# Branch C's output gate of tokens 256-511 computed feature by feature inside the lookup loop, and seven of sixteen lookups weighed by DVE in the first units

## The chip, the cores and the metric

One core of one Trainium2 chip. The metric is the device time of one execution in microseconds; the kernel before was run three times. All arithmetic is in float32: a matrix product of two operands of this type shows in the trace as two MATMUL records (passes).

## What is computed

One layer of a transformer-like trunk on 512 tokens of width 1024:

```
n = adaLN(RMSNorm(x), c)
ya, yb, yc = sparse attention(n), stick-breaking attention(n), gated linear attention(n)
   yc = rms_norm(o) * gain * silu(r),    r = n @ w_cr        (512 columns: the output gate of branch C)
merged = sum_b sigmoid(n @ G_b + bias_b) * (y_b @ w_o_b)
h = x + gate1 * (merged @ w_out)
n2 = adaLN(RMSNorm(h), c)
out = h + gate2 * sum over 8 heads, 16 experts: softmax * gelu(n2 . u[expert]) * v[expert]
```

The last line is the lookup part. Each of the 4 tiles of 128 tokens has 8 heads, and each head picks 16 experts per token out of 16384. A lookup (number n, 0 to 511) gathers one expert for each token of a tile: 128 rows of 8 KB, u and v side by side, 1 MB. 16 lookups of one head and tile are a unit (0 to 31); 4 lookups are a slot (0 to 127) of the order in which all other work is strewn into the loop.

## The kernel before, in words

Everything is written out by hand: each engine runs one long program, and semaphores order them. Stages:

1. Modulation, norm, transposition (to some 95 us), then the projections. `jobs_of_projection` lists the jobs: "d" gives features on partitions, "t" tokens on partitions. Jobs of kind "rc" (slot 7 of the weights, w_proj 7, 2 MB) compute r, one for each tile of 128 tokens, 8 products of 128x128 by 512 columns (L665). Before the change there are four.
2. Branch A for tokens 0-255 (`for it in range(NA + 5)`, 21 turns). `job_after(it)` puts one of the projection jobs after every odd turn, until all but the last four (`LATE = 4`) are done: turns 17 and 19 hold the jobs rc 0 and rc 1. The weights stream through three slots in a fixed order; w_proj 7 takes the slot of w_proj 6 and can be issued by SP only when PE has used that. After turn 17's job come the column sums (L599), 64 narrow products that finish the modulation; in turn 19 branch A's output is turned (L749).
3. Branch B (`for it in range(HB + 2)`) starts with the product of L806. Behind it stand three of the last four jobs (cu 0 and cu 1, the decay projection, L676, and rc 2), and in turn 2 the last (rc 3). Gate and output products of the merge (`gate_product`, L770, and `out_product`, L784), for tokens 0-255, are put between.
4. Branch C for all tokens. Silu of r on ACT (L1393), times the gain on POOL (L2211), times the normed output on DVE (L1878), then PE turns it (L926).
5. The rest of the merge and W_out for tokens 0-255, norm, the first queries.
6. The lookup loop. For each lookup: POOL issues the gather (L2238) into a slot of a ring (8 slots until lookup 120, then 10, up to 15), DVE forms the dot product (L2071), ACT the gelu (L1504), DVE the weight (L2080). Then either PE weighs the row (`weigh`: ACT writes a diagonal matrix, L1515, PE two products of 512 columns, L1121) or DVE does (L2095, two halves of 512). `on_dve(n)` says which: lookups 6, 9, 12, 15 of a unit, and also 1 and 3 in the units 1 to 7 and 9 to 15. The slot of the ring is free when the row is weighed.

Into the loop are strewn, by slot: branch A for tokens 256-511, the queries and scores of further heads (`QUERY_SLOT`: the product in that slot and the next, the score in the second after it; ACT copies it, DVE picks the 16 experts of unit u + 2 in unit u), and the merge for tokens 256-511 (`MERGE_SLOT`, 24 items: branch and 128 features each). A merge item is `merge_products` on PE (8 gate products L1023 into bank 6, 4 output products L1028 into bank 7, 256 columns each), `half_gate` on ACT (Tanh, L1458) and, one slot later, `half_merge` on DVE (L1914 to L1918). SP loads its weights, 768 KB, three items ahead (L538), and the weights of a query, 1152 KB, two slots ahead of it (L532). Pieces of W_out follow in slots 39 to 42.

At the end the last weights and the last weighing are followed by `finish`: bank + DVE's sum (L2110), times gate2 (L2112), plus h (L2115), and a store of 512 KB.

```
def job_after(it):
    return J_A + it // 2 if it % 2 == 1 and J_A + it // 2 < NJ - LATE else None

def half_unit(n):
    return (n // KT + 1) % 3, n % KT
```

Of the kernel before, what the change touches and what calls it, by code (L numbers as in the profile page):

```python
# [7 lines left out]
ALU = mybir.AluOpType  # L8
# [5 lines left out]
P = 128  # L14
# [28 lines left out]
V_C, V_BMOD, V_G1, V_G2, V_BG, V_BA, V_GAIN, V_ONG = 0, 8, 56, 64, 72, 96, 98, 102  # L43
# [59 lines left out]
def jobs_of_projection():  # L103
# [16 lines left out]
def encoder_layer(nc, cst, vec, x, x_turned, w_mod, w_proj, w_small, w_alpha, w_merge, w_out, w_pq,  # L120
                  uv_table, out):
    with ExitStack() as ctx:
# [159 lines left out]
        ON_DVE, ALSO_DVE = (6, 9, 12, 15), (1, 3)  # L282
# [173 lines left out]
        QUERY_SLOT = {(44 if q == 10 else 4 * (q - 3) + 1): q for q in range(3, 11)}  # L456
# [3 lines left out]
        def half_unit(n):  # L460
            return (n // KT + 1) % 3, n % KT
# [15 lines left out]
        def unit_of(t, h):  # L477
# [4 lines left out]
            [4, 7, 8, 11, 12, 15, 16, 19, 20, 22, 23, 24, 26, 27, 28, 29, 30, 31, 32, 33, 34, 35, 36, 37])}  # L482
# [3 lines left out]
        LATE_QUERY_AT = {2: 2, 4: 3}  # L486
# [9 lines left out]
        def _(sp):  # L496
# [37 lines left out]
            def merge_weights(n):  # L534
                br, c = half_unit(n)
                if n >= 3:
                    sp.wait_ge(s["mh_used"], n - 2)
                sp.dma_start(mh_slot[n % 3], w_merge[3 * br + c // 3][:, UNIT_W * (c % 3):UNIT_W * (c % 3 + 1)])\  # L538
                  .then_inc(mh_in[n % 3], 16)
# [22 lines left out]
            for slot in range(NL // GROUP):  # L562
                if slot in MERGE_SLOT and MERGE_SLOT[slot] + 3 < NG:
                    merge_weights(MERGE_SLOT[slot] + 3)
# [5 lines left out]
                if slot == 38:  # L570
                    sp.wait_ge(s["mh_used"], NG)
# [6 lines left out]
            for t in range(TT):  # L578
                sp.wait_ge(s["added"], t + 1)
                sp.dma_start(out[P * t:P * (t + 1), :], h_tm(t)).then_inc(s["stored"], 16)  # L580
            sp.wait_ge(s["stored"], 16 * TT)
# [13 lines left out]
        def _(pe):  # L595
# [375 lines left out]
            def query(q, c):  # L971

                h, lo, n = QUERIES[q]
                if c == 0:
# [5 lines left out]
                    if q == 10:  # L980
                        pe.wait_ge(s["yg_ready"], 8)
# [31 lines left out]
            def merge_products(n):  # L1013

                br, c = half_unit(n)
# [5 lines left out]
                pe.wait_ge(s["gate_ready"], NG + n)  # L1021
                for k in range(KT):
                    mm = pe.matmul(bank(6, H), w[:, P * k:P * (k + 1)], n_t[:, k, H:T],  # L1023
                                   start=(k == 0), stop=(k == KT - 1))
                mm.then_inc(s["gl_done"], 1)
                pe.wait_ge(s["gate_used"], NG + n)
# [7 lines left out]
            def output_piece(p):  # L1034

                pe.wait_ge(wo_in[p % 2], 16 * (p // 2 + 1))
                if p == 0:
                    pe.wait_ge(s["gate_used"], 2 * NG)
                    pe.wait_ge(s["ot_out"], TT)
                    pe.wait_ge(s["q_out"], 10)  # L1040
# [1254 lines left out]
```

## Time and profile before

| | |
|---|---|
| three runs, median (lowest, highest) | 2041.88 us (2039.61, 2043.86) |
| the profiled execution, its time | 2041.46 us |
| its span, first to last instruction | 2039.7 us |
| mean granted TensorE clock | 0.910 of full speed |
| busy: PE, DVE, ACT, POOL | 1670.9, 1443.5, 579.5, 632.1 us |
| moved by DMA | 659.79 MB, of which 536.90 MB by the gathers |

How to read it: the times come from unprofiled and profiled executions; the rows come from one profiled execution, so a sum of rows is set against 2041.46, and what lies outside the span is 1.8 us. Busy shares are means over stages that have different limits.

### The profile page before, as it was taken

How to read it: one execution, taken by the hardware profiler on the slowest of the kernel's cores; microseconds unless marked ns; L12 is line 12 of the kernel's file. 1: busy time of each engine (PE TensorE's matmuls, PEld its weight loads, DVE VectorE, ACT ScalarE, POOL GpSimd, SP SyncE). 2: the span in 40 equal slices, each digit the busy share in tenths (PEclk: the TensorE clock that was granted, in tenths of full speed). 3: DMA queues.
4: the chain of work that ended last, by engine and by line, in shares of the span. 5: the costliest groups of instructions: out<-in, count | busy, mean ns of one | idle time of the engine just before them, and what ended most of it. 6: DMA issues, size and time to landing. Idle time of an engine off the chain costs nothing.

```text
span 2039.7 us, 17878 instructions
## 1 busy us (share of the span) xinstructions
PE 1670.9 (82%) x5626; PEld 946.5 (46%) x5626; DVE 1443.5 (71%) x3353; ACT 579.5 (28%) x1272; POOL 632.1 (31%) x542
## 2 busy tenths in 40 slices
PE   4999989999998898999888867777877676667676
PEld 3533446667786565556555523334433222222222
DVE  5353642668328788887778899878777878887876
ACT  2111114664224253442211223222222222222221
POOL 0000001110003433334333545444444544445441
PEclk8999998999999999999899978878898988888888
DMA  9633020221449999999999999999999999999995
GB/s 375 250 131 118 7 88 10 77 93 57 163 177 372 385 419 419 401 398 406 406 420 420 419 417 405 421 419 419 420 420 421 420 419 420 420 419 419 420 419 228
DMA packets 89183, 659.79 MB, mean 323 GB/s; under 512 B 9968, under 2 KB 10240, under 8 KB 15488
## 3 DMA queue, kind: packets, MB, share of 16 engines
q0 software_dynamic: 73728, 536.90, 63.9%
q1 hardware_dynamic: 14768, 120.75, 15.0%
q8 instruction: 45, 0.74, 0.1%
q10 hardware_dynamic: 592, 0.98, 0.1%
q14 instruction: 50, 0.41, 0.1%
HBM read 655.52 MB, written 2.82 MB: 323 GB/s over the span
## 4 chain that ended last, share of the span: by engine, by line
PE 41%; DMA 34%; DVE 12%; issue 7%; ACT 4%; POOL 2%; SPq 0%; DVEq 0%; POOLq 0%; PEldq 0%; ACTq 0%
DMA sb<-uv_table,sb 33%; PE ps L1121 11%; PE ps L663 6%; PE ps L665 4%; PE ps L770 3%; PE ps L984 3%; DVE sb L2071 2%; DVE sb L2095 2%; POOL sb L2238 2%; PE ps L1023 2%; PE ps L1028 2%; PE ps L784 1%; PE ps L949 1%; DMA sb<-w_mod 1%; PE ps L1047 1%
## 5 line engine op out<-in xcount | busy, mean ns | idle before, releaser
L1121 PE MATMUL ps<-sb 128*128 128x512 f32 x1424 | 774.1, 689 | 273.0 <-ACT sb L1515 269.3
L2238 POOL DMA_INDIRECT sb<-uv_table,sb x512 | 605.1, 1182 | 870.9 <-PE ps L1121 657.4
L2071 DVE CUSTOM_DVE_ANT_0 sb<-sb 128x1024 f32<-128x1024 f32 x512 | 625.2, 1221 | 248.1 <-DMA sb<-uv_table,sb 240.1
L1121 PEld LDWEIGHTS ps<-sb 128*128 128x128 f32 x1424 | 292.3, 217 | 695.2 <-ACT sb L1515 392.0
L1515 ACT ACTIVATE sb<-sb 128x128 f32<-128x128 f32 x356 | 132.0, 397 | 607.1 <-DVE sb L2080 602.1
L2095 DVE SCALAR_TENSOR_TENSOR sb<-sb 128x512 f32<-128x512 f32 x304 | 214.7, 748 | 2.2
L1504 ACT ACTIVATE sb<-sb 128x2 f32<-128x2 f32 x256 | 51.7, 202 | 396.3 <-DVE sb L2071 396.2
L2200 POOL TENSOR_TENSOR sb<-sb 128x128 f32<-128x128 f32 x8 | 13.1, 1636 | 422.8 <-DVE sb L1776 422.8
L663 PE MATMUL ps<-sb 128*128 128x512 f32 (+1 forms) x304 | 125.2, 563 | 0.1
L984 PE MATMUL ps<-sb 128*128 128x256 f32 (+1 forms) x576 | 117.8, 359 | 0.3 <-issue 0.3
L984 PEld LDWEIGHTS ps<-sb 128*128 128x128 f32 x576 | 100.5, 197 | 30.8 <-issue 20.4
L665 PE MATMUL ps<-sb 128*128 128x512 f32 x192 | 93.1, 641 | 6.7 <-DMA sb<-w_proj 6.7
L770 PE MATMUL ps<-sb 128*128 128x256 f32 x384 | 91.5, 392 | 7.0 <-ACT sb L1326 3.0
L1023 PE MATMUL ps<-sb 128*128 128x256 f32 x384 | 87.2, 379 | 2.5 <-ACT sb L1458 2.5
L663 PEld LDWEIGHTS ps<-sb 128*128 128x128 f32 x304 | 57.1, 194 | 62.1 <-issue 55.4
L770 PEld LDWEIGHTS ps<-sb 128*128 128x128 f32 x384 | 73.3, 195 | 20.5 <-ACT sb L1326 3.4
L1023 PEld LDWEIGHTS ps<-sb 128*128 128x128 f32 x384 | 71.5, 189 | 19.9 <-issue 10.7
L665 PEld LDWEIGHTS ps<-sb 128*128 128x128 f32 x192 | 38.7, 206 | 56.2 <-issue 48.4
L1028 PE MATMUL ps<-sb 128*128 128x256 f32 x192 | 51.3, 414 | 14.1 <-DVE sb L1918 13.7
L1566 ACT ACT_TABLE_LOAD x43 | 55.2, 1283 | 0.7
L1028 PEld LDWEIGHTS ps<-sb 128*128 128x128 f32 x192 | 38.8, 207 | 23.5 <-DVE sb L1918 16.8
L1647 DVE SCALAR_TENSOR_TENSOR sb<-sb 128x4096 f32<-128x4096 f32 x7 | 31.4, 4483 | 22.4 <-DMA sb<-w_mod 22.0
(281 smaller groups left out, 1776.7 us busy)
## 6 DMA issues: line engine op xcount, KB each, us to landing
sb<-w_mod SPq DMA_DIRECT2D x11, 2048.0 KB, 9.6
sb<-w_pq SPq DMA_DIRECT2D x18, 1152.0 KB
sb<-w_merge SPq DMA_DIRECT2D x24, 768.0 KB
sb<-w_proj SPq DMA_DIRECT2D x8, 2048.0 KB, 8.9
sb<-w_merge SPq DMA_DIRECT2D x6, 2304.0 KB, 9.0
sb<-w_out SPq DMA_DIRECT2D x8, 1024.0 KB, 10.5
sb<-uv_table,sb POOLq DMA_INDIRECT x512, 27.7
sb<-w_merge SPq DMA_DIRECT2D x3, 1536.0 KB, 6.5
```

The source lines that it names most:

```text
L663: mm = pe.matmul(bank(b, n), w[:, i, k, :], n_t[:, k, 0:n], start=(k == 0), stop=(k == KT - 1))
L665: mm = pe.matmul(bank(b), n_t[:, k, P * i:P * (i + 1)], tiles(views[slot], KT)[:, k, :], start=(k == 0), stop=(k == KT - 1))
L770: mm = pe.matmul(gate_at(n), w[:, P * k:P * (k + 1)], n_t[:, k, 0:H], start=(k == 0), stop=(k == KT - 1))
L984: mm = pe.matmul(bank(6 if q < EARLY_Q else 4, n, H * c), w[:, c, k, :], n_t[:, k, lo:lo + n], start=(k == 0), stop=(k == KT - 1))
L1023: mm = pe.matmul(bank(6, H), w[:, P * k:P * (k + 1)], n_t[:, k, H:T], start=(k == 0), stop=(k == KT - 1))
L1028: mm = pe.matmul(bank(7, H), w[:, P * (KT + k):P * (KT + k + 1)], y_of(br, 1)[:, k, :], start=(k == 0), stop=(k == 3))
L1121: mm = pe.matmul(bank(2 * (t % 2) + f), dgw[m % NDG], row_v(n)[:, T * f:T * (f + 1)], start=(i == 0), stop=(i == PH * PK - 2))
L1515: act.activation(dgw[m % NDG], ident, ACT.Copy, scale=wgt[n // PK % 2][:, n % PK:n % PK + 1])\
L1566: act.activation(warm, cact[:, 0:1], ACT.Gelu)
L2071: dve.tensor_tensor_reduce(out=row_u(n), in0=row_u(n), in1=n2_tm(u // PH), scale=1.0, scalar=0.0, op0=ALU.mult, op1=ALU.add, accum_out=dot ...
L2095: ins = dve.scalar_tensor_tensor(acc_v[f], v, wgt[u % 2][:, i:i + 1], acc_v[f], ALU.mult, ALU.add)
L2238: pool.indirect_dma_start(out=ring[PLACE[n]], out_offset=None, in_=uv_table, in_offset=bass.IndirectOffsetOnAxis(ap=experts[u % 4][:, i:i ...
```

## The change

Five edits, in one version.

- r is projected for tokens 0-255 alone: two of the four "rc" jobs go, and the last four jobs are now rc 0, cu 0, cu 1, rc 1. Silu, gain and product of branch C's end take the first 256 tokens alone. yc of tokens 256-511 is turned without its gate.
- Its gate comes as four new items of the merge list (`ITEMS`, now 28). A gate item loads 512 KB from a new input w_rc, makes 8 products as a merge item does (no output products), Tanh without bias, and two operations on DVE: (tanh + 1) * r from bank 6, then yc = yc * (0.5 * gain) * that. `MERGE_SLOT` is new: gate items in slots 8, 12, 16, 20, each two slots ahead of the next merge item, 28 slots from 6 to 37. Before, it held 24 slots from 4 to 37. Branch 2 (yc) comes after the gates.
- Queries 8, 9, 10 (tokens 128-255 of heads 0 to 2) move from slots 21, 25, 44 to 42, 46, 50. Late query 2 moves from slot 2 to 3.
- In units 1 to 7 DVE weighs lookups 1, 3, 6, 9, 11, 13, 15 (7 of 16), in the last unit 2, 5, 8, 10.
- The end: gelu, weight and diagonal of the last two lookups are made singly. DVE multiplies its own sum by gate2 and adds h while the last rows come (`own_part`, `own_rest`), and `finish_last` works and stores in two halves of 512 columns.

```diff
-    jobs += [("t", 7, t, "rc", None) for t in range(TT - 2)]
+    jobs += [("t", 7, 0, "rc", None)]
     jobs += [("u", None, i, "cu", None) for i in range(2)]
-    jobs += [("t", 7, t, "rc", None) for t in range(TT - 2, TT)]
+    jobs += [("t", 7, 1, "rc", None)]
...
+        ON_DVE, ALSO_DVE, LAST_DVE, FIRST_DVE = (6, 9, 12, 15), (1, 3), (2, 5, 8, 10), (1, 3, 6, 9, 11, 13, 15)
...
+            if u == NU - 1:
+                return i in LAST_DVE
+            if 0 < u < PH:
+                return i in FIRST_DVE
             return i in ON_DVE or (i in ALSO_DVE and u % PH > 0 and n < 2 * PH * PK)
...
-        QUERY_SLOT = {(44 if q == 10 else 4 * (q - 3) + 1): q for q in range(3, 11)}
+        QUERY_SLOT = {(4 * q + 10 if q >= 8 else 4 * (q - 3) + 1): q for q in range(3, 11)}
...
-        def half_unit(n):
-            return (n // KT + 1) % 3, n % KT
+        ITEMS = [(1, 0), (1, 1)] + [e for c in range(3) for e in (("gate", c), (1, 2 * c + 2), (1, 2 * c + 3))] + [("gate", 3)] + [(2, c) for c in range(KT)] + [(0, c) for c in range(KT)]
...
-            [4, 7, 8, 11, 12, 15, 16, 19, 20, 22, 23, 24, 26, 27, 28, 29, 30, 31, 32, 33, 34, 35, 36, 37])}
+            [6, 7, 8, 10, 11, 12, 14, 15, 16, 18, 19, 20, 22, 23, 24, 25, 26, 27, 28, 29, 30, 31, 32, 33, 34, 35, 36, 37])}
...
-        LATE_QUERY_AT = {2: 2, 4: 3}
+        LATE_QUERY_AT = {3: 2, 4: 3}
...
+                if br == "gate":
+                    sp.dma_start(mh_slot[n % 3][:, 0:KT * P], w_rc[:, KT * P * c:KT * P * (c + 1)]).then_inc(mh_in[n % 3], 16)
...
+                if br == "gate":
+                    y = y_of(2, 1)[:, c, :]
+                    done(dve.scalar_tensor_tensor(gates_h[n % 2], gates_h[n % 2], 1.0, bank(6, H), ALU.add, ALU.mult))
+                    dve.scalar_tensor_tensor(y, y, vcol(V_OGC + c), gates_h[n % 2], ALU.mult, ALU.mult).then_inc(s["gate_used"], 1)
...
-            act.activation(area("rc", 0, TT * T), area("rc", 0, TT * T), ACT.Silu).then_inc(s["rsil"], 1)
+            act.activation(area("rc", 0, 2 * T), area("rc", 0, 2 * T), ACT.Silu).then_inc(s["rsil"], 1)
...
+            def finish_last():
+
+                t = TT - 1
+                dve.wait_ge(s["weighed"], by_pe(NL))
+                for f in range(2):
+                    dve.tensor_tensor(acc_v[f], bank(2 * (t % 2) + f), g2row[:, T * f:T * (f + 1)], ALU.mult).then_inc(v_step, 1)
+                v_count[0] += 2
+                for f in range(2):
+                    half = slice(T * f, T * (f + 1))
+                    dve.wait_ge(v_step, v_count[0] - 1 + f)
+                    dve.tensor_tensor(h_tm(t)[:, half], acc_v[f], acc_tmp[:, half], ALU.add).then_inc(s["added"], 1)
```

## Rows read from the trace of the kernel before

**Rows 1.** Stretches of the lookup loop: length, busy, PEclk, DMA share, GB/s.

```profile
core 0: us, PE busy (x) PEld busy (x) DVE busy (x) ACT busy (x) POOL busy (x), PEclk, DMA share, GB/s
671.50:2028.30 1356.80, 1059.93 (x2953) 553.67 (x2954) 1088.66 (x2704) 362.97 (x932) 581.71 (x492) 0.89 1.00 412
...
720.50:767.40 46.90, 44.40 (x174) 28.05 (x173) 39.31 (x105) 24.24 (x51) 17.69 (x16) 1.00 1.01 419
...
813.60:861.70 48.10, 44.60 (x158) 27.40 (x157) 40.14 (x105) 19.54 (x43) 16.99 (x16) 0.96 0.99 400
861.70:913.30 51.60, 47.09 (x206) 30.90 (x204) 40.54 (x106) 24.01 (x50) 17.19 (x16) 1.00 0.98 399
...
960.50:1012.80 52.30, 44.92 (x156) 29.74 (x157) 39.86 (x98) 11.69 (x31) 19.85 (x16) 0.90 1.01 404
```

**Rows 2.** Waits from 671 to 1110 us: in total, times, longest.

```profile
POOL sb L2238 <- PE ps L1121: 221.2, 66, 11.4
...
DVE sb L2071 <- DMA sb<-uv_table,sb: 69.0, 54, 5.1
```

**Rows 3.** The chain of waits from 279 to 345: start, us, what.

```profile
286.81 8.38 DMA sb<-w_proj
...
295.23 8.56 PE ps L665 x16
303.78 9.18 PE ps L599 x64
...
313.91 9.28 PE ps L665 x16
...
323.96 2.39 PE ps L806 x8
...
328.26 8.77 PE ps L665 x16
```

**Rows 4.** Timeline, the last product of branch A on PE.

```profile
287.23 1.30 PE L740 MATMUL ps<-sb 128*128 128x64 f32 x8
```

**Rows 5.** Timeline of DVE at the end.

```profile
2026.93 0.16 DVE L2080 TENSOR_TENSOR sb<-sb 128x2 f32<-128x2 f32 x1
...
2028.45 1.22 DVE L2071 CUSTOM_DVE_ANT_0 sb<-sb 128x1024 f32<-128x1024 f32 x1
...
2032.76 1.29 DVE L2110 TENSOR_TENSOR sb<-ps,sb 128x512 f32<-128x512 f32 x2 [1.20 <-PE ps L1121]
```

**Rows 6.** Stretches behind the column sums and near the end (columns as rows 1).

```profile
313.00:324.00 11.00, 10.22 (x21) 4.51 (x20) 0.61 (x4) 1.20 (x2) 0.00 (x0) 0.75 0.00 0
...
2018.30:2028.50 10.20, 8.22 (x10) 2.88 (x10) 7.71 (x15) 1.50 (x5) 0.00 (x0) 0.51 0.06 24
```

**Rows 7.** Timeline, where PE turns branch C's output.

```profile
538.71 1.97 PE L926 MATMUL ps<-sb 128*128 128x128 f32 x16 [0.57 <-ACT sb L1326]
```

**Rows 8.** DMA issues by line: count, KB each.

```profile
sb<-w_pq SPq DMA_DIRECT2D x18, 1152.0 KB
sb<-w_merge SPq DMA_DIRECT2D x24, 768.0 KB
```

**Rows 9.** Two late units, with a w_pq load and without (columns as rows 1).

```profile
1495.30:1539.00 43.70, 32.47 (x88) 16.91 (x88) 32.97 (x85) 10.01 (x28) 20.41 (x17) 0.92 1.01 419
1584.10:1625.00 40.90, 23.93 (x48) 9.13 (x48) 32.87 (x85) 9.52 (x27) 21.71 (x20) 0.96 1.01 420
```

**Rows 10.** Groups by form, 671.5 to 1110: busy us, mean ns, idle before.

```profile
L1023 PE MATMUL ps<-sb 128*128 128x256 f32 x384 | 87.2, 379 | 2.5 <-ACT sb L1458 2.5
L2095 DVE SCALAR_TENSOR_TENSOR sb<-sb 128x512 f32<-128x512 f32 x102 | 72.0, 748 | 0.6
...
L1028 PE MATMUL ps<-sb 128*128 128x256 f32 x192 | 51.3, 414 | 14.1 <-DVE sb L1918 13.7 <-DVEq L1915 0.3
...
L984 PE MATMUL ps<-sb 128*128 128x128 f32 x64 | 8.2, 283 | 0.0
...
L1917 DVE SCALAR_TENSOR_TENSOR sb<-sb,ps 128x256 f32<-128x256 f32 x16 | 6.6, 412 | 0.9 <-DVE sb L2035 0.9
```

**Rows 11.** The chain from 990 to 1012, three lookups in a row on PE.

```profile
995.50 5.16 PE ps L1121 x12
```

More of the change, by code:

```diff
@@ L562, in _ @@
             for slot in range(NL // GROUP):
-                if slot in MERGE_SLOT and MERGE_SLOT[slot] + 3 < NG:
+                if slot in MERGE_SLOT and MERGE_SLOT[slot] + 3 < NM:
                     merge_weights(MERGE_SLOT[slot] + 3)
@@ L576, in _ @@
                     out_weights(PIECE_SLOT[slot] + 2)
-            for t in range(TT):
+            for t in range(TT - 1):
                 sp.wait_ge(s["added"], t + 1)
                 sp.dma_start(out[P * t:P * (t + 1), :], h_tm(t)).then_inc(s["stored"], 16)
-            sp.wait_ge(s["stored"], 16 * TT)
+            for f in range(2):
+                sp.wait_ge(s["added"], TT + f)
+                sp.dma_start(out[P * (TT - 1):T, T * f:T * (f + 1)], h_tm(TT - 1)[:, T * f:T * (f + 1)]).then_inc(s["stored"], 16)
+            sp.wait_ge(s["stored"], 16 * (TT + 1))
         def arrived(eng, kind, i):
@@ L1021, in merge_products @@
                 pe.wait_ge(s["gate_ready"], NG + n)
+                if n >= 1 and ITEMS[n - 1][0] == "gate":
+                    pe.wait_ge(s["gate_used"], NG + n)
                 for k in range(KT):
@@ L1121, in weigh @@
                     mm = pe.matmul(bank(2 * (t % 2) + f), dgw[m % NDG], row_v(n)[:, T * f:T * (f + 1)],
-                                   start=(i == 0), stop=(i == PH * PK - 2))
+                                   start=(i == 0), stop=(i == PH * PK - (2 if t < TT - 1 else 1)))
                 mm.then_inc(s["weighed"], 1)
@@ L1456, in half_gate @@
                     act.wait_ge(s["gate_used"], NG + n - 1)
-                br, c = half_unit(n)
-                act.activation(gates_h[n % 2], bank(6, H), ACT.Tanh, scale=0.5, bias=half_bias[:, KT * br + c:KT * br + c + 1])\
-                   .then_inc(s["gate_ready"], 1)
+                br, c = ITEMS[n]
+                bias = 0.0 if br == "gate" else half_bias[:, KT * br + c:KT * br + c + 1]
+                act.activation(gates_h[n % 2], bank(6, H), ACT.Tanh, scale=0.5, bias=bias).then_inc(s["gate_ready"], 1)
             def gated_piece(p):
@@ L1516, in diagonals, with last_one @@
                        .then_inc(s["dg_ready"], 1)
+            def last_one(n):
+                i = n % PK
+                act.wait_ge(s["dot_done"], n + 1)
+                act.activation(gelu[(NU - 1) % 2][:, i:i + 1], dots[(NU - 1) % 2][:, i:i + 1], ACT.Gelu).then_inc(s["gelu_ready"], 1)
+                m = by_pe(n)
+                act.wait_ge(s["weighed"], m - NDG + 1)
+                act.wait_ge(s["w_ready"], NL // 2 + n - (NL - 2))
+                act.activation(dgw[m % NDG], ident, ACT.Copy, scale=wgt[(NU - 1) % 2][:, i:i + 1]).then_inc(s["dg_ready"], 1)
             def late_exp(j):
@@ L1555, in _ @@
                     late_y(LATE_Y[slot - 1])
-                for pair in range(max(EARLY // 2, 2 * slot), 2 * slot + 2):
+                for pair in range(max(EARLY // 2, 2 * slot), min(2 * slot + 2, NL // 2 - 1)):
                     gelus(pair)
@@ L1590, in _ @@
                     tokens_out(m)
+            last_one(NL - 2)
+            last_one(NL - 1)
         @block.vector
@@ L1742, in _ @@
             dve.tensor_scalar(half_bias, vcol(V_BG, NG), 0.5, None, ALU.mult)
+            done(dve.tensor_scalar(vcol(V_OGC, 4), vcol(V_OGC, 4), 0.5, None, ALU.mult))
             dve.tensor_scalar(half_gt1, mcol(GT1, KT), 0.5, None, ALU.mult).then_inc(s["halved"], 1)
@@ L2165, in _ @@
                     weigh(n - 2)
+                if n == NL - 3:
+                    own_part()
+                if n == NL - 2:
+                    own_rest()
                 for part in PICK_AT[i] if u + 2 < NU else ():
@@ L2186, in _ @@
                     dve.tensor_copy(g2row, ps[:, 2 * T:2 * T + D]).then_inc(s["g2_ready"], 1)
-            weights(NL // 2 - 1)
-            weigh(NL - 1)
-            finish(TT - 1)
+            weight_one(NL - 1)
+            finish_last()
         @block.gpsimd
```

62 lines of the change are left out of this document (42 added, 20 removed).

## The prediction

> **What bounds the kernel now.** I read the stretches of the lookup loop first, then its waits, then the chain of work in the stage ahead of the loop and at the end. From 671.5 to 2028.3 us, two thirds of the span, the DMA engines are busy all the time (share 1.00, 412 GB/s), while PE and DVE are busy in 78 and 80% [rows 1]. So in the loop the sum of transferred bytes sets the time. The units of 16 lookups that lie early are near a second bound: where PE is busy 44 to 47 us of 47 to 52, the rate falls from 419 to 399 GB/s [rows 1]. There POOL waits 221 us for PE to give back ring slots, and DVE 69 us for rows [rows 2]: the queue of gathers is short, and sometimes a DMA engine runs dry. Ahead of the loop no gathers run, and PE's chain counts. At 286.8 PE needs w_proj 7, whose load can only then be issued; it waits 8.38 us, does rc product 0 (8.56), column sums (9.18), turns branch A's output, does rc product 1 (9.28), and starts branch B only at 323.96 [rows 3]. At the end DVE takes the last row at 2028.45, waits for PE until 2032.76, then takes 3.8 us in three steps, and the store follows [rows 5].
>
> **The change, part by part.** The profiled execution took 2041.46 us (span 2039.7 and 1.8 around it), 0.42 under the median of 2041.88; the sum is made against 2041.46.
>
> 1. Two of the four rc products go, and with two jobs fewer none falls on turns 17 and 19 of branch A's loop. Gone from the chain: wait 8.38, product 8.56, product 9.28, together 26.2 us [rows 3]. What is late next: the column sums then wait for PE's last product of branch A, which ends at 288.5 [rows 4], 1.7 after 286.8; the copy that stands ahead of B's start is replaced by that of branch A's turned output, 0.2 more. w_proj 7 lands at 295.2, under the column sums, which now run from 288.5 to 297.9, and rc product 0 wants it only after 301. So -24.3. The last four jobs remain four (rc0, cu0, cu1, rc1 for cu0, cu1, rc2, rc3) with the same work inside branch B: 0. SP's queue keeps its order; the next merge load, behind w_proj 7, is wanted 13 us after B's start.
>
> 2. The clock. In the 11 us behind the column sums the granted clock is 0.75 on average [rows 6]: half of them at 1.2 GHz. Now B's first product (2.39) and rc product 0 stand there. The first at half rate costs 2.4 more, rc0 then about 0.5; rc2 in this place took 8.77 instead of the 7 of the undisturbed products [rows 3], so 1.7 comes back. +1.2, bounds -1.7 and +5.
>
> 3. Branch C's tail: Silu, POOL's gain and DVE's product do half. DVE's product ends 1 us earlier at most, but PE starts its turn at 538.71 held by the Tanh of a gate product [rows 7]. 0; if that cover were gone, -1.
>
> 4. Four gate items in the loop. Bytes: a w_pq load of 1152 KB [rows 8] lengthens a unit from 40.9 to 43.7 us, 2.8 us [rows 9], so 2.43 us for 1000 KB. Three gate loads of 512 KB fall into the loop, the fourth ahead of it in place of a merge load, which moves in (768 KB [rows 8]): 2304 KB, +5.6. The bytes are certain and the engines have no free time [rows 1], so this is the firmest term in the loop. The page "DMA: Bandwidth & Descriptors" of the Trainium skill (Specifications) gives a core 358 GB/s from HBM; by that the term would be an estimated 6.6 us, but this trace holds 412 to 420 GB/s, so the row decides.
> PE: 16 passes, 3.6 us (384 passes of L1023 take 87.2 in 24 items); ACT a Tanh of a piece of 256; DVE two operations of 0.41 [rows 10]. Each item stands in a unit of its own, units 2 to 5.
>
> 5. FIRST_DVE: one lookup more on DVE in units 1 to 7. Per unit PE -1.7 (12 passes of L1121, three lookups, take 5.16 [rows 11]), DVE +1.5 (two of 0.748 [rows 10]). DVE has 7.6 us idle in the 46.9 of unit 2 [rows 1]; with the gate item's 0.8 it keeps 5. PE in units 2 to 4: +3.6 - 1.7 = +1.9 in a unit that the bytes make 1.25 longer; it is idle 2.5 in unit 2 and 3.5 in unit 4 [rows 1]. That is covered, barely: 0.5 us of new starving in all.
>
> 6. Queries 8 and 9 leave units 5 and 6 (slots 21, 25) for slots 42, 46, and query 10 goes from 44 to 50; their loads follow (2 x 2.8 us, moved, not added). One merge item goes from unit 5 to 6. Unit 5 has the worst rate, 399 of 420: 2.6 us lost in 51.6. On PE it loses 1.7 of lookups, 2.1 of an output product (192 passes, 51.3) and 4.1 of a query (32 passes) [rows 10], and 2.8 us of DMA: I give back all 2.6, and 0.5 of the 2.0 that the unit at 960.5 loses (404 of 420) [rows 1]. Unit 4 loses 2.3 by the same sum and keeps it, as it gets a gate item. Bounds of the whole: +6 (three units starve 2 each) and -9 (all is regained). Term: -3.1 + 0.5 = -2.6. In the new place each score is copied one slot before its pick; DVE waits some 1.3 us there for two diagonals and a copy on ACT, in units 11 to 13. From lookup 120 on the ring has ten slots and more in place of eight, so the gathers are queued deeper and it costs 0; uncovered it would be 4. Late query 2 one slot later: 0.
>
> 7. The end. Now the lookups 12 to 15 of the last unit are all PE's. The weights of 12 and 13 come at 2027.1 [rows 5], their diagonals let PE start at 2028.0, four lookups of 1.72 end at 2034.9. PE's clock is 0.51 from 2018.3 to 2028.5 [rows 6]; I let one of the four run at half rate: 2036.6, 3.9 later than 2032.7. DVE then has four operations on half rows (2.7) in place of 3.8, as half of the finish is done before the last row, and the last store is half as large (256 KB, -0.6). +2.2; bounds +0.5 (full clock) and +7 (all four at half rate).
>
> Sum: -24.3 + 1.2 + 5.6 - 2.6 + 2.2 = -17.9; 2041.46 - 17.9 = 2023.6, at the median 2024.0. A measurement here tells about 0.2% (4 us) from no change.
>
> **The rivals.** (a) Only the products go and not the wait of 8.38, because the column sums are held by something that the trace doesn't show: -17.8 in place of -24.3, 2030. Against it: the sums read what DVE added up from the eight mod2 loads ahead of branch A, and in the chain they stand behind a product of PE and nothing else. 0.07. (b) PE's clock: branch B's first 12 us all run at 1.2 GHz; twice 2.39 + 1.91 + 7 less what is counted gives +5 and 2029. For it: the 0.75 of [rows 6]. The page "TensorE: Matmul & The Clock Gate" of the Trainium skill (Part 1) says that half rate is the default and sustained work lifts it; taking work away speaks for this rival. 0.08. (c) The early units starve more: three units lose 3 us each and nothing is regained, 2024 + 9 + 2.6 = 2035.6. For it: POOL's 221 us for PE [rows 2], PE at 95%. 0.12. (d) Slower: the gate items are not hidden at all. Place: units 1 to 7, with a ring of eight slots. Price: 4 x (3.6 + 0.5 + 0.8) + 7 x 1.5 = 30 us in place of the -2.6, 2057 (0.5 for the Tanh). It decides from the point at which PE or DVE needs more than the unit's 47 to 50 us; both stay under by 1.5 to 5. 0.04. (e) Everything starved is regained (-9 in place of -2.6) and the end runs at full clock: 2016. 0.13. The forecast has 0.56.
>
> **How the numbers follow.** 2024 is the likeliest. From 2015 to 2032 lie the forecast with its bounds, (a), (b) and (e); (c) and (d) lie outside with 0.16. Only (d) is above 2042, and a stronger (c) may come to within 4 us: faster 0.93, same 0.03, slower 0.04.
>
> **What the profile of the changed kernel would show.** Branch B's first product at about 299.7 in place of 323.96, with no wait for w_proj before it; if it stands later than 304, term 1 failed. The first gather 23 us earlier too. The stretch from the first unit to the last row longer by 3 us; the unit with the worst rate at 415 GB/s or more; if units 2 to 4 fall under 400, (c) holds. PE's last product 6 to 9 us after the last row landed (now 4.3), DVE's rest 2.7. The forecast is wrong if the branch B start moves by less than 18 us or the loop grows by over 10.

## The result, and the profile after

| | before | after |
|---|---|---|
| median (lowest, highest) of 16 runs each | 2041.18 us (2039.07, 2045.04) | 2049.38 us (2046.25, 2059.97) |
| ratio, 95% interval | | 1.0045 (1.0036 to 1.0054) |
| span of the profiled execution | 2039.7 us | 2047.4 us |
| first gather issued | 614.2 us | 592.3 us |
| first dot product of unit 1, of unit 7 | 671.5, 960.5 us | 648.3, 958.6 us |
| last dot product starts | 2028.45 us | 2034.31 us |

The changed kernel is 8.2 us slower by the medians (9.2 by the ratio), where 17.2 us less were forecast. In the profile the loop starts 21.9 us earlier. By unit 7 that lead is down to 1.9 us; by the last dot product it is a lag of 5.9, and the end adds the rest of 7.7.

The chain of waits of the kernel after, from the column sums on (start, us, what; [rows 3] before):

```profile
288.39 9.64 PE ps L609 x64
...
299.67 4.63 PE ps L816 x8
304.30 9.74 PE ps L675 x16
314.04 1.91 PE ps L686 x4
315.95 3.65 PE ps L780 x16
```

L609 are the column sums, L816 is branch B's first product, at 299.67 as forecast and with no wait for a load ahead of it. It stands wholly at half clock (4.63 us where the same product takes 2.35 further down the chain; the granted clock from 299.7 to 304.3 is 0.50), product 0 of r behind it (L675) in part (0.72). The gate product L780 behind them comes 21.1 us earlier than in the kernel before (337.03 there) and not 24.3.

Stretches of the loop after (length, busy, PEclk, DMA share, GB/s; [rows 1] before): the whole loop from unit 1, then units 2, 3, 4, 5 and 6, and units 1 to 6 together.

```profile
648.30:2034.30 1386.00, 1062.26 (x2986) 558.94 (x2985) 1105.70 (x2732) 362.34 (x929) 573.35 (x491) 0.89 0.99 405
...
699.80:754.30 54.50, 48.09 (x185) 31.39 (x185) 41.56 (x109) 24.43 (x51) 17.57 (x16) 0.97 0.95 380
754.30:802.70 48.40, 44.87 (x176) 29.86 (x176) 38.87 (x98) 18.19 (x41) 16.97 (x16) 0.96 1.00 406
802.70:857.30 54.60, 48.92 (x169) 29.95 (x169) 42.20 (x108) 19.74 (x43) 17.71 (x16) 0.94 0.96 373
857.30:906.90 49.60, 41.29 (x155) 24.89 (x155) 41.90 (x108) 23.09 (x48) 17.57 (x16) 0.97 1.01 416
906.90:958.60 51.70, 43.11 (x164) 28.89 (x164) 40.67 (x100) 14.21 (x33) 17.76 (x16) 0.96 0.97 382
648.30:958.60 310.30, 268.99 (x995) 171.78 (x993) 244.55 (x622) 115.02 (x253) 106.46 (x95) 0.96 0.98 388
```

The last of these in the kernel before:

```profile
671.50:960.50 289.00, 263.88 (x1024) 169.00 (x1024) 233.37 (x603) 116.10 (x258) 108.79 (x96) 0.98 1.00 411
```

Units 1 to 6 take 310.3 us and not 289.0, at 388 GB/s and not 411. Units 2 and 4 are the worst, at 54.5 and 54.6. PE has only 5 us more work in the six units than before and is idle for 41 us of them, not 25: the amount of its work doesn't explain 21 us, so the question is when it works. The waits from unit 1 to unit 9 (648 to 1107 us; in total, times, longest; [rows 2] before):

```profile
POOL sb L2308 <- PE ps L1138: 261.3, 59, 12.1
...
PE ps L1045 <- DVE sb L1952: 24.9, 9, 4.9
```

POOL's gathers (L2308) wait 40 us more for PE's weighings (L1138), in fewer and longer waits; the stretch itself is 20 us longer. The second row is PE's own wait: an item's output products (L1045) want the bank that DVE has not yet read out for the item ahead (L1952). It was 13.7 us before [rows 10]; in units 1 to 6 alone it is 6.8 us, against 1.3.

Timeline of the end after ([rows 5] before):

```profile
2033.55 8.72 PE L1138 MATMUL ps<-sb 128*128 128x512 f32 x16 [1.36 <-ACT sb L1532]
...
2034.31 1.22 DVE L2105 CUSTOM_DVE_ANT_0 sb<-sb 128x1024 f32<-128x1024 f32 x1
...
2042.31 1.29 DVE L2175 TENSOR_TENSOR sb<-ps,sb 128x512 f32<-128x512 f32 x2 [6.35 <-PE ps L1138]
```

PE gives back the last lookup 8.0 us after the last dot product has begun; it was 4.3.

### The profile page after: what moved, and what is told of

Same layout as the page of the kernel before. It is cut to its first block, busy times and chain, and to the rows that moved or that the text cites. A ratio compares the mean times of both kernels' runs of the same rounds, so it can differ in the third digit from the quotient of the medians.

```text
span 2047.4 us, 17941 instructions
## 1 busy us (share of the span) xinstructions
PE 1661.3 (81%) x5630; PEld 946.9 (46%) x5630; DVE 1457.1 (71%) x3380; ACT 577.4 (28%) x1268; POOL 623.1 (30%) x542
## 4 chain that ended last, share of the span: by engine, by line
DMA 37%; PE 35%; DVE 15%; issue 7%; ACT 3%; POOL 2%; DVEq 0%; SPq 0%; POOLq 0%; ACTq 0%
DMA sb<-uv_table,sb 36%; PE ps L1138 9%; PE ps L673 6%; DVE sb L2105 4%; PE ps L675 3%; PE ps L780 3%; DVE sb L2129 3%; POOL sb L2308 2%; PE ps L994 2%; PE ps L1045 2%; PE ps L1035 2%; PE ps L794 1%; DMA sb<-w_mod 1%; PE ps L609 1%; PE ps L959 1%
## 5 line engine op out<-in xcount | busy, mean ns | idle before, releaser
L1138 PE MATMUL ps<-sb 128*128 128x512 f32 x1396 | 762.2, 690 | 282.2 <-ACT sb L1532 277.3
L2308 POOL DMA_INDIRECT sb<-uv_table,sb x512 | 598.3, 1169 | 907.5 <-PE ps L1138 702.5
L1138 PEld LDWEIGHTS ps<-sb 128*128 128x128 f32 x1396 | 286.3, 217 | 700.5 <-ACT sb L1532 399.4
L2129 DVE SCALAR_TENSOR_TENSOR sb<-sb 128x512 f32<-128x512 f32 x318 | 224.9, 749 | 1.9
L1521 ACT ACTIVATE sb<-sb 128x2 f32<-128x2 f32 x255 | 51.5, 202 | 377.9 <-DVE sb L2105 377.8
L2270 POOL TENSOR_TENSOR sb<-sb 128x128 f32<-128x128 f32 x8 | 13.1, 1636 | 402.0 <-DVE sb L1806 402.0
L994 PE MATMUL ps<-sb 128*128 128x256 f32 (+1 forms) x576 | 118.8, 361 | 1.6 <-ACT sb L1481 1.1
L994 PEld LDWEIGHTS ps<-sb 128*128 128x128 f32 x576 | 100.6, 196 | 31.5 <-issue 20.3
L1035 PE MATMUL ps<-sb 128*128 128x256 f32 x448 | 101.6, 379 | 0.4 <-ACT sb L1476 0.4
L780 PE MATMUL ps<-sb 128*128 128x256 f32 x384 | 89.9, 387 | 7.0 <-ACT sb L1343 3.0
L1035 PEld LDWEIGHTS ps<-sb 128*128 128x128 f32 x448 | 83.8, 189 | 21.9 <-issue 11.1
L780 PEld LDWEIGHTS ps<-sb 128*128 128x128 f32 x384 | 72.0, 192 | 20.3 <-ACT sb L1343 3.4
L1045 PE MATMUL ps<-sb 128*128 128x256 f32 x192 | 53.5, 427 | 28.1 <-DVE sb L1952 24.9
L675 PE MATMUL ps<-sb 128*128 128x512 f32 x160 | 75.8, 629 | 0.0
L1045 PEld LDWEIGHTS ps<-sb 128*128 128x128 f32 x192 | 39.6, 212 | 39.4 <-DVE sb L1952 28.5
L675 PEld LDWEIGHTS ps<-sb 128*128 128x128 f32 x160 | 31.6, 202 | 40.0 <-issue 39.1
L1676 DVE SCALAR_TENSOR_TENSOR sb<-sb 128x4096 f32<-128x4096 f32 x7 | 31.4, 4484 | 22.3 <-DMA sb<-w_mod 21.9
```

The costliest lines, as they stand in the source:

```text
L675: mm = pe.matmul(bank(b), n_t[:, k, P * i:P * (i + 1)], tiles(views[slot], KT)[:, k, :], start=(k == 0), stop=(k == KT - 1))
L780: mm = pe.matmul(gate_at(n), w[:, P * k:P * (k + 1)], n_t[:, k, 0:H], start=(k == 0), stop=(k == KT - 1))
L994: mm = pe.matmul(bank(6 if q < EARLY_Q else 4, n, H * c), w[:, c, k, :], n_t[:, k, lo:lo + n], start=(k == 0), stop=(k == KT - 1))
L1045: mm = pe.matmul(bank(7, H), w[:, P * (KT + k):P * (KT + k + 1)], y_of(br, 1)[:, k, :], start=(k == 0), stop=(k == 3))
L1138: mm = pe.matmul(bank(2 * (t % 2) + f), dgw[m % NDG], row_v(n)[:, T * f:T * (f + 1)], start=(i == 0), stop=(i == PH * PK - (2 if t < TT - ...
L2129: ins = dve.scalar_tensor_tensor(acc_v[f], v, wgt[u % 2][:, i:i + 1], acc_v[f], ALU.mult, ALU.add)
```

## The experiments

All ratios are to the kernel before, run on the same chip beside each; 0.001 is 2.04 us. "Units 1 to 6" goes from the first dot product of unit 1 to that of unit 7, in the profiled execution. The interval stands behind each ratio, some 0.0008 to 0.0018 to either side, so a difference of two ratios is known to 3 or 4 us. One profiled execution can lie 4 or 5 us from the median of its kernel, and a difference of one or two us between two traces means little.

### First batch: one part of the change back at a time

DVE's share. The rule for units 1 to 7 is taken out of the changed kernel, and put alone into the kernel before:

```diff
-            if 0 < u < PH:
-                return i in FIRST_DVE
```

> The changed kernel with one edit undone: in units 1 to 7 DVE weighs six of sixteen lookups again. The changed kernel stands at 1.0045 of before. Theory S (the seventh weighing keeps DVE from its rows and delays the release of ring slots in units 1 to 6, which together grew by 18 us): the ratio falls to 0.997 or less, units 1 to 6 shorter by 10 us or more. Theory G (the gate items on PE do it): PE has 1.7 us more per unit, the ratio rises to 1.006 or more. Theory L (late query 2 one slot later): no change, 1.0045.

> The kernel before with one edit of the change: DVE weighs lookups 1, 3, 6, 9, 11, 13, 15 in units 1 to 7. Theory S: slower, by 4 us or more, ratio 1.002 to 1.008. Theory G: PE is relieved by 1.7 us per unit, ratio 0.996 to 1.000.

Measured: 1.0011 (0.9999 to 1.0024), units 1 to 6 306.6 us; and on the kernel before 1.0028 (1.0016 to 1.004), units 1 to 6 295.4 in place of 289.0. The seventh lookup on DVE costs 7 us in the one kernel and 6 in the other. The prediction had 0.5.

The late query back in slot 2:

```diff
-        LATE_QUERY_AT = {3: 2, 4: 3}
+        LATE_QUERY_AT = {2: 2, 4: 3}
```

> The changed kernel with late query 2 back in slot 2. Theory L (its product now ends one slot before late query 3, whose weights SP loads only after it, and PE waits for that load): PE's wait of about 4 us ahead of L1074 in slot 4 goes, unit 1 shorter by 2 to 5 us, ratio 1.002 to 1.0035. Theories S and G: that wait goes too but units 2 to 6 stay as long, at least 12 us over those of before.

Measured: 1.0047 (1.003 to 1.0065), as the change. The trace of the change has a wait of PE for the late query's weights in slot 4 (L1074, 4.0 us) which is not in the trace before. In this run's trace it is gone, as expected, but unit 1 is only 0.7 us shorter (50.8 against 51.5) and the time is the same: removing a 4 us wait of PE gave nothing.

The gate items and their slots taken out (this kernel leaves out branch C's output gate of tokens 256-511), the other items in the slots that the change gives them (6, 7, 10, 11, 14, 15, 18, 19, ...):

```diff
-        ITEMS = [(1, 0), (1, 1)] + [e for c in range(3) for e in (("gate", c), ...
+        ITEMS = [(1, 0), (1, 1)] + [(1, c) for c in range(2, KT)] + ...
-            [6, 7, 8, 10, 11, 12, 14, 15, 16, 18, 19, 20, 22,
+            [6, 7, 10, 11, 14, 15, 18, 19, 22,
```

> The changed kernel without its four gate items and without their weights; the other items keep their slots. It leaves out branch C's output gate of tokens 256-511. Theory G (PE and ACT time of the gate items starves the ring): units 2 to 5 shorter by 12 us or more together, ratio 0.993 to 0.998, far more than the 5 us that the bytes cost. Theory S: only the bytes come back, ratio about 1.002.

Measured: 1.003 (1.0018 to 1.0041). Only 3 us came back; unit 2 still took 51.7 and unit 4 56.4 us. The changed kernel's loop has lost 20 us by unit 11 (553.4 us for units 0 to 10, 533.3 before); DVE's share with 7 and the gate items with 3 make half of it. Left to explain were units 2 and 4, and what else had moved there was the place of the merge items.

### Second batch: the slots

The kernel before has merge items in slots 4, 8, 12, 16 and the change in 6, 10, 14, 18. A query's two halves stand in slots 5 and 6, 9 and 10, 13 and 14, 17 and 18: so the change puts a merge item right behind a query's second half.

Without gate items (and so without that gate, as above), in the old slots:

```diff
-            [6, 7, 10, 11, 14, 15, 18, 19, 22, 23, 24, 25, 26,
+            [4, 7, 8, 11, 12, 15, 16, 19, 20, 22, 23, 24, 26,
```

> The changed kernel without its four gate items (left out: branch C's output gate of tokens 256-511), and with the 24 merge items in the slots of the kernel before (4, 7, 8, 11, 12, 15, 16, 19, ...), where the run without gate items had them at 6, 7, 10, 11, 14, 15, 18, 19. Theory of placement: slots 6, 10, 14, 18 also hold half of a query's product (3.65 us on PE), slots 4, 8, 12, 16 hold none; a query half and a merge item (5 us) in one slot put PE behind, and POOL waits for ring slots. Then units 2 and 4, 51.7 and 56.4 us there, become some 6 us shorter each (46 to 50), units 1 to 6 together fall from 308 to 293-298, and the ratio to before is 0.993 to 0.996. Rival, it is the number of bytes or DVE's extra lookups alone: units 1 to 6 stay within 3 us of 308 and the ratio within 0.001 of 1.003.

Measured: 0.996 (0.9947 to 0.9973), units 1 to 6 295.7. Against the run without gate items in the new slots that is 14 us, from the slots alone. Its unit 2, with the same unit in the new slots ahead of it:

```profile
699.40:751.10 51.70, 46.15 (x169) 28.42 (x169) 40.85 (x107) 24.05 (x50) 15.34 (x16) 0.93 0.96 385
```

```profile
701.90:750.30 48.40, 44.49 (x177) 28.75 (x177) 40.61 (x108) 23.94 (x50) 18.46 (x16) 1.00 1.00 405
```

Gate items back, in slots 5, 9, 13, 17 between the merge items of the old slots, and the same with DVE's old share:

```diff
+        ITEMS = [e for c in range(4) for e in ((1, 2 * c), ("gate", c), (1, 2 * c + 1))] + ...
+            [4, 5, 7, 8, 9, 11, 12, 13, 15, 16, 17, 19, 20, 22, 23, 24, 26,
```

> The whole change, its computation complete, but merge items in the slots of the kernel before and the gate items at slots 5, 9, 13, 17, each between two merge items. Theory of placement: the pair query half with merge item is gone, but slots 5, 9, 13, 17 have a query half and now a gate item (2.9 us): units 1 to 6 at 296 to 304, ratio 0.995 to 0.999. Rival (placement is nothing): units 1 to 6 at 307 to 313, ratio 1.0035 to 1.0055.

> As the run with gate items at 5, 9, 13, 17, and DVE's share of units 1 to 7 as in the kernel before. DVE's seventh lookup cost 0.0034 with the new slots and 0.0028 in the kernel before; if the two causes add, this is 0.003 below that run: 0.992 to 0.996, faster than both kernels. If placement was the only reason for which the seventh lookup hurt, it is equal to that run within 0.001.

Measured: 1.003 (1.002 to 1.004), units 1 to 6 304.4, at the edge of the expected stretch and above the expected ratio: the gate items now stand with the query's first half. With DVE's old share 0.997 (0.996 to 0.9981), so the seventh lookup costs 12 us here, against 6 and 7 in the other two kernels. So the causes don't simply add; that this one costs most here isn't explained, since in the changed kernel PE is later still and it cost 7.

The constants' length, 16 columns more in place of 4:

> The changed kernel, only the vector of constants grows by 16 columns (64 bytes a partition) and not by 4 (16 bytes), so that all that lies behind it in the SBUF is at the alignment of the kernel before. Theory: late units take 40.98 us in place of 40.89 because rows of the ring start at 16 bytes off; then they return to 40.89 and the time falls by 2 to 4 us, ratio 1.0025 to 1.0035. Rival, alignment is nothing: 1.0045 within 0.001 and 40.98 stays.

Measured: 1.005 (1.0036 to 1.0064), late units still at 40.98 us in place of 40.89. Alignment is not it. Why a late unit takes 0.09 us longer (1 to 2 us in all) stays open; it does in every version with the change's new input, also where no gate item is. All of these also lack two products of r, so the input isn't singled out.

### Third batch: the slots alone, the products of r alone

The kernel before with one line changed:

```diff
-            [4, 7, 8, 11, 12, 15, 16, 19, 20,
+            [6, 7, 10, 11, 14, 15, 18, 19, 20,
```

> The kernel before with one line changed: its first eight merge items of the loop stand in slots 6, 7, 10, 11, 14, 15, 18, 19 and not in 4, 7, 8, 11, 12, 15, 16, 19. Nothing else is moved. Theory of placement: units 1 to 4 lengthen from 190 to 200-206, ratio 1.004 to 1.0075. Rival, the placement hurts only together with the other edits: ratio within 0.001 of 1.

Measured: 1.0086 (1.007 to 1.0101), 17.6 us slower, more than expected. Its units 2 and 4, and units 1 to 6 together:

```profile
723.00:777.80 54.80, 47.09 (x172) 29.18 (x171) 39.46 (x105) 24.56 (x51) 16.49 (x16) 0.91 0.92 366
...
822.80:880.30 57.50, 49.54 (x165) 29.68 (x164) 40.22 (x105) 19.95 (x43) 17.64 (x17) 0.88 0.92 360
...
672.10:980.20 308.10, 273.37 (x1024) 173.42 (x1024) 233.66 (x602) 116.97 (x258) 105.76 (x96) 0.94 0.96 385
```

The matmuls are as many as in the kernel before (1024), the units have the same merge items each, and 19 us are gone. Its chain of waits, in unit 2 (L984 a query's half, L1023 and L1028 a merge item, L1135 a score of branch A, L1121 weighings):

```profile
744.16 1.64 PE ps L1135 x2
745.80 4.93 PE ps L984 x16
750.74 3.44 PE ps L1121 x8
754.18 0.61 PE ps L1158 x6
754.79 0.34 PE ps L1146 x3
755.13 1.72 PE ps L1121 x4
756.85 0.84 PE ps L1135 x2
757.69 3.65 PE ps L984 x16
761.34 3.45 PE ps L1023 x16
764.79 1.75 PE ps L1028 x8
766.54 0.14 issue
766.67 1.96 PE ps L1121 x4
```

From 744 on the chain never leaves PE. From 756.85 to 766.67 it is one block of 9.8 us in which PE weighs nothing. POOL's next gather, and the stretch of the DMA engines behind it (0.98 and 389 GB/s in the ten us ahead of it, 1.01 and 418 in the ten behind):

```profile
769.41 0.94 POOL L2238 DMA_INDIRECT sb<-uv_table,sb  x1 [11.35 <-PE ps L1121]
```

```profile
765.00:775.00 10.00, 9.85 (x40) 5.61 (x39) 5.13 (x13) 3.30 (x7) 4.21 (x5) 1.00 0.70 236
```

POOL issues nothing for 11.35 us because PE has given no slot back, and the DMA engines then run dry for 3 of 10 us. An estimate of what the ring can bridge: the DMA engines bring a lookup in 2.6 us (16 in 40.9, [rows 9]), a ring of eight is 20 us of transfers, and a gather in this chain took 13.1 us to land, so some 7 are left.

Seven is no sharp limit. In PE's timelines of units 1 to 6 the stretches of more than 7 us between two weighings, with other products in them, add up to 82 us in the kernel before (10 of them, the longest 9.9), to 115 here (13, longest 11.7), to 132 in the changed kernel (15, longest 11.0), and to 89 and 125 in the two runs without gate items, in the old slots and the new. Of all kernels in this document that keep whole blocks, those with 79 to 98 us of them take 289 to 296 us for the six units, those with 105 to 113 us 298 to 304, and those with 115 and more 307 to 314. A few such stretches are borne, then. Here, in unit 2 and again in unit 4, two of nearly 10 us begin within 17 us of each other; the three of over 9 us in the kernel before stand in three different units. That it is this closeness which empties the ring is a reading of the timelines and wasn't tested by itself.

The first edit alone: two jobs of r left out and no gate items in their place (branch C's output gate of tokens 256-511 is left out), the rest as before.

> The kernel before with the first edit alone: two of the four products of r are left out, and r's part for tokens 256-511 (branch C's output gate of these tokens is left out and no gate items take its place); merge slots, queries, DVE's share and the end are those of before. Term 1 and its clock stand alone: first gather at 592 in place of 614, the lookup loop as before (units 0 to 10 at 533 us within 3). Theory: 22 us less, ratio 0.989 within 0.001. Rival, an earlier start of the loop is given back by the loop itself whatever stands in it (the bytes bound the whole): ratio above 0.993.

Measured: 0.9909 (0.9893 to 0.9924), 18.6 us faster; first gather at 591.8, units 0 to 10 536.1 us, 2.9 more than before. Term 1 is real, and the loop gives some 4 us of it back.

Two more from the version at 0.997: its gate items late, in slots 17, 18, 20, 21; and, by itself, the old end (gate items at 5, 9, 13, 17):

```diff
+        ITEMS = [(1, c) for c in range(7)] + [("gate", 0), ("gate", 1), (1, 7), ("gate", 2), ("gate", 3)] + ...
+            [4, 7, 8, 11, 12, 15, 16, 17, 18, 19, 20, 21, 22, 23, 24, 25, 26, 27, 28, 29,
```

> As the run with gate items at 5, 9, 13, 17 and DVE's old share (0.997), but the gate items wait until slots 17, 18, 20, 21, when most early query work is over (one merge item stays at 19, branch C's items follow from 22). Theory of placement: units 1 to 4, which took 203.8 us there and 190.1 in the kernel before, fall to 190 to 194; units 4 and 5 take the gates at 1 to 2 us each; ratio 0.992 to 0.995. Rival, a gate item costs its bytes and its work wherever it stands: 0.997 within 0.001.

> As the run with gate items at 5, 9, 13, 17 and DVE's old share (0.997), with the end of the kernel before: DVE weighs 6, 9, 12, 15 of the last unit, one finish after the last weighing, one store of 512 KB. If the new end costs what the traces of before and after show (last unit and rest 48.75 to 51.7 us), it falls by 2 to 3 us: ratio 0.9955 to 0.996. Rival, the traces differ by chance and the new end is as good: 0.997.

Measured: 1.007 (1.0057 to 1.0083) for the late gates, a clear miss. Units 1 to 3 did fall, but unit 5 took 65.5 us. Its stretch and its chain (L1033 and L1043 an item's products, L1944 DVE's second operation of a gate item, L1136 weighings):

```profile
844.40:909.90 65.50, 55.94 (x190) 36.72 (x190) 41.27 (x108) 24.30 (x50) 16.98 (x16) 0.85 0.84 323
```

```profile
870.88 0.50 DVE sb L1944
871.37 0.14 issue
871.51 6.68 PE ps L1033 x16
...
889.69 0.50 DVE sb L1944
890.19 0.14 issue
890.32 5.80 PE ps L1033 x16
```

DVE reads a gate item's bank one slot later, and an item in the very next slot wants that bank: PE stands still until DVE is through. That is what two slots between a gate item and the next one are for, and I had given it up. After the stand (2.6 and 4.1 us) PE's products run at half clock or nearly so, 6.68 and 5.80 us in place of 3.45, at a granted clock of 0.55 and 0.63.

The old end: 0.9972 (0.9957 to 0.9987), no different from 0.997. In the profiles the last unit and the rest are 2.1 us shorter with it (48.8 against 50.9), less than the runs can tell.

### Fourth batch: the blocks cut in two

Every item keeps its slot. On PE its products stand between the second and the third lookup of the slot, and not behind the query's half:

```diff
-                if slot in MERGE_SLOT:
-                    merge_products(MERGE_SLOT[slot])
...
                     if n % GROUP == 2:
+                        if slot in MERGE_SLOT:
+                            merge_products(MERGE_SLOT[slot])
                         amid(slot)
```

> The changed kernel, every item in its slot, but on PE the products of a merge or gate item stand between the second and the third lookup of the slot and not behind the query's half ahead of the first. Block theory: the 9 us in which PE weighs no lookup fall into two of 4 to 5 us with lookups between, the eight-slot ring bridges them: units 1 to 6 fall from 310 to 295-300 and the ratio from 1.0045 to 0.997-0.999. Rival, density: PE is short of time over the two slots whatever the order; units 1 to 6 stay within 3 us of 310, ratio 1.003 to 1.006.

> Control: the kernel before, merge products between the second and the third lookup of their slot, nothing else. In it only a few merge items share a slot with a query's half or score. Block theory: little to gain, ratio 0.997 to 1.000. Rival, any order with shorter blocks helps the short ring everywhere: 0.993 to 0.996.

Measured on the changed kernel: 0.9961 (0.9947 to 0.9975), 17 us faster than the change and now faster than before. On the kernel before: 0.9993 (0.9984 to 1.0001), nothing. So it isn't the amount of work in two or three slots but its being in one piece. The kernel before had nothing to gain, though its stretches over 7 us went from 10 to none (its longest from 9.9 to 6.7 us): what it had of them cost nothing that the runs can tell. Units 2 and 4 and units 1 to 6 of the changed kernel with its blocks cut:

```profile
699.30:750.00 50.70, 47.45 (x186) 30.82 (x185) 41.26 (x109) 24.46 (x51) 19.23 (x16) 0.97 0.99 396
...
796.20:849.80 53.60, 48.74 (x170) 30.64 (x170) 42.40 (x108) 19.74 (x43) 19.06 (x17) 0.94 0.98 391
...
648.10:946.90 298.80, 268.82 (x1007) 173.16 (x1005) 244.52 (x623) 115.42 (x253) 115.16 (x97) 0.97 1.00 401
```

and the chain in its unit 2 (L994 a query's half, L1138 weighings, L1035 and L1045 a merge item):

```profile
730.01 3.65 PE ps L994 x16
733.66 1.72 PE ps L1138 x4
735.38 3.46 PE ps L1035 x16
738.84 1.75 PE ps L1045 x8
```

One lookup is weighed between the two halves of the block: the other of the first two is DVE's. PE is as busy in the six units as in the change (268.8 and 269.0 us), and they take 11.5 us less. POOL's longest wait for PE fell from 12.1 to 8.4 us.

The edit does a second thing: PE comes to a bank two lookups later, so DVE has more time to read it out, and PE's waits for that (L1045 in units 1 to 6, 10.0 us in the change, 6.8 of them for L1952) are gone. In this pair of runs that can't be told from the cutting of the blocks. In the next pair it nearly can: there such waits were 2.1 us uncut.

The queries 8, 9, 10 back in slots 21, 25, 44 (gate items at 5, 9, 13, 17, old share, old end), and that with the blocks cut:

> As the run with gate items at 5, 9, 13, 17, DVE's old share and the old end (0.9972), with queries 8, 9, 10 back in slots 21, 25, 44. Prediction's term 6: leaving units 5 and 6 regained 2.6 us, so this is 2.6 us slower, 0.9985. Rival by the unit lengths (units 11 and 12 gained 5.2 us, units 5 and 6 lost 4.5 and more): 1 to 2 us faster, 0.9962 to 0.9967.

> As the run with the queries back, and on PE the products of a merge or gate item between the second and third lookup of their slot. Block theory: gate items in the slots of a query half cost only their bytes, units 1 to 4 fall from 203 to 193-196: ratio 0.990 to 0.9935. Density: no change, within 0.001 of the run with the queries back.

Measured: 0.9973 (0.9963 to 0.9983), against 0.9972 with the queries moved: neither expectation. With the blocks cut 0.9938 (0.9923 to 0.9952), 7 us less, and units 1 to 6 at 295.7 in place of 303.6 us, the PE clock at full speed in all six:

```profile
646.60:942.30 295.70, 275.12 (x1098) 180.00 (x1097) 237.32 (x610) 117.42 (x262) 109.72 (x97) 1.00 1.01 412
```

That is the rate of the kernel before (411), with the gate items' bytes and work in it. Of the 7.9 us only some 2 can be PE's waits for DVE; the rest is the cutting.

### Fifth batch: which version to keep

The change's own slots with the blocks cut, DVE's old share and the old end; and gate items at 5, 9, 13, 17 with the blocks cut and the queries moved:

> The changed kernel with its own slots and moved queries, merge and gate products between the lookups of their slot (0.9961), DVE's old share in units 1 to 7 and the old end. If DVE's seventh lookup costs by loading DVE, whatever PE does, 0.003 comes back, and 0 to 0.001 by the end: 0.9925. Rival: it cost only because PE's blocks held the ring; then 0.9955 to 0.996.

> The version at 0.9938 (gates at 5, 9, 13, 17, split blocks, old share, old end) with queries 8, 9, 10 moved to 42, 46, 50 as in the change. If moving them regains starving in units 5 and 6 (term 6): 0.9925. If their bytes only move and there is nothing to regain once blocks are split: 0.9938 to 0.9945.

Measured: 0.9944 (0.9931 to 0.9957), 2028.5 us; and 0.9936 (0.9923 to 0.9948). Three versions between 0.9936 and 0.9944 can't be told apart. All compute the whole layer and are 11 to 13 us faster than the kernel before and some 21 faster than the change. Once the blocks are cut, it no longer matters in which of the two sets of slots the items stand, nor where the queries are. DVE's old share and the old end together gave 0.0017 here, between the two expectations: as measured, the share costs 6 to 12 us where the blocks are whole and 3 or 4 at most where they are cut, but with some 4 us of doubt on each of these differences the link is likely rather than shown.

## Why the prediction was wrong

The step that failed is the count by units in terms 5 and 6. It allowed the early units +6 us at most and expected -2.6, from the room that PE and DVE have in a whole unit ("That is covered, barely: 0.5 us of new starving in all") and from which unit an item falls into ("One merge item goes from unit 5 to 6"). The runs show in its place that two edits cost by where they put work inside a unit: the merge items' new slots, right behind a query's half, 17.6 us alone on the kernel before, and the seventh lookup on DVE 6 to 12 us.

The kernels form one path from before to after, each step the difference of two ratios, known to 3 or 4 us:

| step | ratio after it | us |
|---|---|---|
| two products of r less, nothing in their place | 0.9909 | -18.6 |
| gate items at 5, 9, 13, 17 (a late query moved with them, worth 0) | 0.9973 | +13 |
| queries 8, 9, 10 moved | 0.9972 | 0 |
| new end | 0.9970 | 0 |
| seven lookups on DVE in units 1 to 7 | 1.0030 | +12 |
| all items in the change's slots | 1.0045 | +3 |

Taken in another order the steps have other sizes (the slots first: +17.6, without gate items +14, last +3), because three of them act on one thing, PE's lateness against a ring of eight slots. No single one of the three can be called the larger part of the loss.

**Term 1 (-24.3)** held at its place, 299.67; that it held to the tenth is luck, as the column sums took 0.46 us longer than before (9.64) and the pieces around them 0.4 less. Rival (a), that only the products would go, is out: the wait of 8.38 went too.

**Term 2 (+1.2)** was 3.2. Branch B's first product took 4.63 us, as forecast (2.39 and 2.4), but product 0 of r took 9.74, 2.8 more than at full clock (6.89 for the last one), where I had given it 0.5. This lies within the bounds. Rival (b) wanted 5.

**Term 3 (0)** held: branch C's output begins to be turned at 516.7 us, 22.0 earlier than [rows 7].

**Term 4 (+5.6 for bytes, the rest covered)** is right for the changed kernel and not in general. In the change's own slots, in which no query's half or score stands, the gate items cost 3 us (1.0030 to 1.0045), no more than their bytes. At 5, 9, 13, 17, beside a query's half, they cost 13, and with the blocks cut 5.9 (0.9909 to 0.9938; the 0.9909 is of an uncut kernel). So the cover failed only where the item stood with other work, a block of 7 us (3.65 and 3.45), and in the changed kernel this term isn't what went wrong.

**Term 5 (+0.5)** failed: 6 to 12 us. I added up PE's work by unit (45 to 47 us of 47 to 50) and found room. Over six units the room was there: the version at 0.9938 does 275.1 us of PE's work in 295.7. But the ring has room for two slots of lookups, not for a unit. DVE, too, had time left in every unit. Each half-row weighing on DVE stands ahead of dots and weights that PE needs; ACT's waits for DVE's weights, 181 us and at most 5.1 in the kernel before, are 210 and at most 6.8 in the change over the same stretch (620 to 1090). With the slots moved alone they stay at 177, so this is the share's mark and not the slots'. That these delays are what costs is argued from those rows; what the runs show is the cost itself.

**Term 6 (-3.1, with term 5's +0.5 the -2.6 of the sum)** was 0 for the queries. Units 11 and 12 grew by 5.2 us, where I had called 4 us covered, and units 5 and 6 gave back no more: 4.9 us, in the pair of runs that differ in the queries alone. The sentence in it that mattered most was the one on merge items: I counted that one goes from unit 5 to 6 and never laid the new slots beside `QUERY_SLOT`. The move from 4, 8, 12, 16 to 6, 10, 14, 18 costs 17.6 us by itself, three times the upper bound of 6 that I allowed.

**Term 7 (+2.2)** held in the trace: PE's last product 8.0 us after the last dot (forecast 6 to 9), DVE's rest 2.5 (2.7), the stretch 2.9 longer. In the runs' times it can't be seen. What delays the last rows was there before and stayed: from 2018.3 to 2028.5 the DMA share is 0.06 [rows 6], and in the changed kernel from 2024 to 2034 it is the same. That is one sixteenth, and reads as one DMA engine that is behind the fifteen others and lands its part of the last rows alone. Why it is behind isn't known.

**The rivals.** The mechanism was that of (c), starving of the early units, and its sign in the profile came true: units 2 and 4 at 380 and 373 GB/s. Its price, three units at 3 us, was far too low, since it was set by how much the units lost already and not by what a block can hold up. Rival (d), the one on the slower side, came nearest with 2057 against 2049.4, mostly by luck: it wanted 20 us for the gate items, which cost 3, and 10.5 for DVE's share, which cost 7 and was priced about right; the slots, which it doesn't name, fill the gap. The forecast's own mark for being wrong, a loop longer by over 10, was met: 26.7 us from the first dot product to the start of unit 31.

## What to carry to other kernels

When work is strewn into a loop that is fed through a ring of buffers, look at how often, and how closely behind one another, an engine gives no buffer back for longer than the ring can bridge; a budget over a whole unit can show room and still miss 20 us. Lay the slots of all strewn tables side by side (queries, merge items, what other engines answer a slot later), and cut long pieces with the loop's own work rather than look for a free slot. If a change moves several tables at once, run the old places with the new work first: here the one-line move cost 17.6 us by itself, and another move of one call, the order within a slot, turned the change into a gain.

## What the runs showed of the hardware

A stall of PE is followed by slow products. Where PE had stood waiting, its next products ran at 1.2 GHz, wholly or in part: 6.68 and 5.80 us in place of 3.45 behind stands of 2.6 and 4.1 us, and 4.93 in place of 3.65 for a query's half behind one of 3.6 (granted clock 0.55, 0.63 and 0.68). The trace agrees with the Trainium skill here ("TensorE: Matmul & The Clock Gate", Part 1), which has the half rate as the default and the full one as what sustained work earns.

How much of the loss this makes is open. It is tempting to say that a late PE makes the DMA engines run dry, the missing rows let PE stand, and it comes back at half speed and later still. Over units 1 to 6 the granted clock was 0.98 before, 0.96 after, 0.94 with the slots moved alone (0.88 in its unit 4), and 1.00 in the version at 0.9938. But the kernel without gate items at 0.9909 had 0.95 and took 290.8 us for the six units, and the version at 0.9936 had 0.95 and took 297.2. A low clock there goes with time in which PE has nothing to do, and by itself it doesn't make the loop slow.

The DMA engines held 412 GB/s over the 1357 us of the loop before, and with the slots moved alone, in ten us around the end of one block of PE, 236 (DMA share 0.70). What lies between the two is how regularly ring slots come back.
